# One core, a hybrid encoder layer: the order of splits, gates and tables around the first two expert blocks

## The reference

```
def block_fn(args):
    tok, w, e = args
    xb = h_pad[tok]                                    # 128 rows of one expert
    gu = xb @ w_gate_up[e]                             # 1024 x 1024
    y = (jax.nn.silu(gu[:, :D_EXPERT]) * gu[:, D_EXPERT:]) @ w_down[e]   # 512 x 1024
    return y * w[:, None]
```

## Time and profile before

| | |
|---|---|
| median of 3 runs | 1258.5 us (1257.77 to 1258.85) |
| the profiled execution | 1256.18 us, span 1254.5 us, granted clock 0.991 |
| TensorE matmuls busy | 1220.5 us, 97% of the span |
| VectorE / ScalarE / GpSimd busy | 904.5 / 610.1 / 218.6 us |
| chain that ended last | PE 91%, DVE 3%, DMA 2%, issue 2% |

### The profile page before, as it was taken

One profiled execution on the slowest core, in us unless ns is written; L12 is line 12 of the kernel. 1 busy time (PEld: TensorE's weight loads), 2 busy tenths in 40 slices (PEclk: granted clock), 3 DMA queues, 4 the chain that ended last, 5 costly groups with the idle time before them and its releaser, 6 DMA issues.

```text
span 1254.5 us, 25280 instructions
## 1 busy us (share of the span) xinstructions
PE 1220.5 (97%) x7475; PEld 1007.7 (80%) x7476; DVE 904.5 (72%) x1137; ACT 610.1 (49%) x665; POOL 218.6 (17%) x281
## 2 busy tenths in 40 slices
PE   5999999999999999999999999999999999999897
PEld 4889999998888865788888888888888888888653
DVE  2546345667999888856887566745889888998497
ACT  3331111131222244647775565645777877787433
POOL 0042311000111111211121111111121221222122
PEclk8999999999999999999999999999999999999999
DMA  9944411046333578767998666955999999998994
GB/s 313 303 140 128 124 48 35 18 135 184 123 115 131 193 287 314 317 257 284 373 402 346 263 260 247 344 221 210 384 405 400 397 395 400 388 401 303 342 404 165
DMA packets 122710, 329.21 MB, mean 262 GB/s; under 512 B 12888, under 2 KB 44704, under 8 KB 122660
## 3 DMA queue, kind: packets, MB, share of 16 engines
q1 hardware_dynamic: 107700, 288.08, 61.6%
q0 software_dynamic: 13088, 34.13, 7.7%
q10 hardware_dynamic: 1872, 6.29, 1.3%
HBM read 296.97 MB, written 39.39 MB: 268 GB/s over the span
## 4 chain that ended last, share of the span: by engine, by line
PE 91%; DVE 3%; DMA 2%; issue 2%; SPq 1%; ACT 1%; POOL 0%; POOLq 0%; DVEq 0%; ACTq 0%
PE bank L1668 22%; PE bank L1670 22%; PE bank L1669 22%; PE bank L1681 4%; PE bank L1683 4%; PE bank L1682 3%; PE bank L1983 3%; PE bank L1898 1%; PE bank L2100 1%; PE bank L2099 1%; PE bank L2023 1%; PE bank L1737 1%; PE bank L1764 1%; PE bank L1728 1%; PE bank L1876 1%
## 5 line engine op out<-in xcount | busy, mean ns | idle before, releaser
L1510 DVE TENSOR_TENSOR gu_l<-gu_raw,gu_h (+1 forms) x128 | 287.3, 2285 | 40.7 <-ACT gu_h L995 27.5
L995 ACT ACTIVATE gu_h<-gu_raw (+1 forms) x128 | 239.1, 1927 | 12.5 <-issue 8.8
L1668 PE MATMUL bank<-gu_h,xT_h 128*128 x608 | 240.3, 395 | 1.3 <-DVE xT_l L1536 1.3
L1670 PE MATMUL bank<-gu_h,xT_l 128*128 x608 | 237.1, 390 | 0.0
L1669 PE MATMUL bank<-gu_l,xT_h 128*128 x608 | 236.5, 389 | 0.0
L1514 DVE TENSOR_TENSOR dn_l<-dn_raw,dn_h (+1 forms) x64 | 143.6, 2285 | 6.7 <-issue 5.0
L1668 PEld LDWEIGHTS bank<-gu_h,xT_h 128*128 128x128 f32 x608 | 114.2, 188 | 24.2 <-issue 2.0
L1670 PEld LDWEIGHTS bank<-gu_h,xT_l 128*128 128x128 f32 x608 | 114.1, 188 | 24.3
L1669 PEld LDWEIGHTS bank<-gu_l,xT_h 128*128 128x128 f32 x608 | 114.3, 188 | 22.6
L1668 PE MATMUL bank<-dn_h,aT_h 128*128 (+1 forms) x308 | 123.2, 400 | 0.0
L1681 PE MATMUL bank<-hT_h,win_h 128*128 128x256 f32 x384 | 110.6, 288 | 11.5 <-DVE hT_l L1188 10.4
(11 more groups left out here) (313 smaller groups left out, 2069.8 us busy)
## 6 DMA issues: line engine op xcount, KB each, us to landing
gu_raw<-in_w_gate_up SPq DMA_DIRECT2D x128, 1024.0 KB, 7.4
dn_raw<-in_w_down SPq DMA_DIRECT2D x64, 1024.0 KB, 7.3
y<-y_rows SPq DMA_DIRECT2D x22, 512.0 KB, 7.3
ada_raw<-in_w_ada SPq DMA_DIRECT2D x20, 512.0 KB, 7.6
ada_raw<-in_w_ada SPq DMA_DIRECT2D x10, 1024.0 KB, 5.5
win_raw<-in_w_in SPq DMA_DIRECT2D x8, 768.0 KB, 9.0
h_rows<-h SPq DMA_DIRECT2D x12, 512.0 KB, 2.7
fin<-x_rows SPq DMA_DIRECT2D x12, 512.0 KB, 9.9
```

What stands on the lines that cost most here:

```text
L995: nc.scalar.activation(gu_slot(gu_h, e, c), gu_slot(gu_raw, e, c), ACT.Copy).then_inc(S["gu_split_h"], 1)
L1510: nv.tensor_tensor(gu_slot(gu_l, e, c), gu_slot(gu_raw, e, c), gu_slot(gu_h, e, c).bitcast(F32), ALU.subtract).then_inc(S["gu_split_l"], 1)
L1668: mm(out, lh, rh, start=start, stop=False)
L1670: return mm(out, ll, rh, start=False, stop=stop)
```

## The change

Four things are done. TensorE turns block 1's rows behind chunk 1 of block 0 and no longer behind chunk 2. In block 0 chunk 3 of the next expert is split before `silu`/`gate` and no longer behind. In block 1 VectorE splits chunk 2 of the next expert behind `gate` and `low_xT`; `scatter_table()` moves from behind `low_xT(2)` to behind the two `low_dn`, and `weights()` behind the whole loop. The tile `x0T_h` starts 64 bytes later.

```diff
--- before.py
+++ after.py
@@ -305,7 +305,7 @@
         aT_h = r.take("aT_h", [P, KE, P], F32R)
         aT_l = r.take("aT_l", [P, KE, P], F32R)
         WT0 = r.at
-        x0_at = C0 + 17728
+        x0_at = C0 + 17792
         r = Region(x0_at)
         x0T_h = r.take("x0T_h", [P, KD, P], F32R)
         x0T_l = r.take("x0T_l", [P, KD, P], F32R)
@@ -1062,13 +1062,14 @@
                     act.wait_ge(S["x1_stored"], 16 * NT)
                     high_xT(1)
                     with act.If(e < e_next):
-                        high_gu(e_next, 2)
+                        for c in (2, 3):
+                            high_gu(e_next, c)
                     act.wait_ge(S["g2_added"], 16)
                 silu(i)
                 if not first:
                     high_xT(i + 1)
-                with act.If(e < e_next):
-                    high_gu(e_next, 3)
+                    with act.If(e < e_next):
+                        high_gu(e_next, 3)
                 if first:
                     for c in range(2):
                         high_dn(0, c)
@@ -1567,21 +1568,19 @@
             def expert_block(i, first=False, second=False):
                 e, e_next = expert_of(i), expert_of(i + 1)
                 with dve.If(e < e_next):
-                    for c in range(2 if first else 3):
+                    for c in range(2 if first or second else 3):
                         low_gu(e_next, c)
                 if first:
                     low_xT(1)
                     with dve.If(e < e_next):
-                        low_gu(e_next, 2)
+                        for c in (2, 3):
+                            low_gu(e_next, c)
                 gate(i)
                 if not first:
                     low_xT(i + 1)
-                if second:
-                    scatter_table()
-                with dve.If(e < e_next):
-                    low_gu(e_next, 3)
-                if second:
-                    weights()
+                    with dve.If(e < e_next):
+                        for c in ((2, 3) if second else (3,)):
+                            low_gu(e_next, c)
                 if first:
                     for c in range(2):
                         low_dn(0, c)
@@ -1589,12 +1588,15 @@
                     with dve.If(expert_of(i - 1) < e):
                         for c in range(2):
                             low_dn(e, c)
+                if second:
+                    scatter_table()
                 low_aT(i)
 
             expert_block(0, first=True)
             expert_block(1, second=True)
             with dve.Fori(2, n_blocks) as i:
                 expert_block(i)
+            weights()
 
             last_block = dve.value_load(block_n[0:1, 1:2], min_val=NE - 1, max_val=MAXBLK - 1)
             last_col = dve.value_load(block_c[0:1, bass.ds(last_block, 1)], min_val=0, max_val=COLS - 1)
@@ -1995,7 +1997,7 @@
                             kk = 2 * c + k
                             last = three(ps[5 + b][:], x0T_h[:, kk, :], x0T_l[:, kk, :], w_h[:, k, n], w_l[:, k, n], kk == 0, kk == KD - 1)
                     last.then_inc(S["gu_used"], 1)
-                    if c == 2:
+                    if c == 1:
                         x_transposes(1)
 
             def gate_up(i, e, chunks=range(4)):
```

## The result

After the change the median is 1263.78 us (1262.01 to 1266.14, 7 runs); the kernel before, run beside it, stands at 1258.5 us (1254.49 to 1260.73, 7 runs). The ratio is 1.0045 with a 95% interval of 1.0029 to 1.0061: 5.7 us slower (3.6 to 7.7). The forecast was 1268.2 us within 1263.5 to 1271.5. The direction and the place were right, the size was too large: the time lies 0.3 us inside the low end.

A forecast was written before the change was run, and what follows sets the result against it. TensorE, busy 97% of the span, was taken to bound the kernel. To the median of 1258.5 us were added 5.6 (table), 1.9 (clock) and 2.2 (tail), 9.7 in all: 1268.2 us, range 1263.5 to 1271.5.

The forecast's parts named there:

- the case without a low clock: Rival: same wait ahead of block 1's down matmuls, clock stays high, tail free; 1264.3 us, chance 0.06.
- the anchor: The forecast's starting point: 1258.5 us, the median of before, 2.3 us above its profiled execution of 1256.18.
- Entry wait: Loop entry: TensorE's 1.30 us wait for block 2's xT_l goes away, as xT_l ends at 514.83.
- Gathered rows: Block 0: block 1's gathered rows land at 490.9, before TensorE needs them at 491.8; no cost.
- Scatter table, +5.6: Block 1: table ends 6.6 us later, at 526.53, so the down matmuls start 5.6 us later, at 535.54.
- the 0.24 us of the tile: Moving x0T_h's start by 64 bytes saves 5 ns on each of 48 matmuls, 0.24 us.
- Clock, +1.9: Behind the new wait TensorE runs at 1.2 GHz for 3.73 us and loses 1.9 us.
- Weights in the tail, +2.2: Tail: GpSimd holds the second operation of weights(), so the tail's first matmul starts 2.2 us later.
- free tail: Rival: same wait and low clock, but GpSimd doesn't hold the tail's small operations, 0.2 us there; 1266.2 us, chance 0.27.

The follow-up runs named there:

- tables_late: Kernel before with scatter_table() and weights() moved behind the two low_dn of block 1, ahead of low_aT(1), nothing else; ratio to before 1.0045, 1263.22 us.
- after_free: Kernel after with the clearing write given its own zeros and semaphore, so take_y(0) doesn't wait for it; ratio to before 1.0008, 1257.62 us.
- turn_only: Kernel before with x_transposes(1) behind chunk 1 in place of chunk 2, nothing else; ratio to before 0.9993, 1257.28 us.
- warm: Kernel after with block 2 written out in TensorE's program and its 8 row transposes made seven times; ratio to before 1.0024, 1262.18 us.
- weights_only: Kernel before with weights() moved behind the loop, nothing else; ratio to before 1.0000, 1258.22 us.
- after_again: The unchanged kernel after, measured once more beside the variants; ratio to before 1.0046, 1262.91 us.
- table_back: Kernel after with scatter_table() alone put back behind low_xT(2), ahead of the splits of chunks 2 and 3; ratio to before 1.0011, 1259.72 us.
- table_mid: Kernel after with scatter_table() behind the splits of chunks 2 and 3, ahead of block 1's two low_dn; ratio to before 1.0023, 1261.9 us.
- order_only: Kernel before with only the split of expert 2's chunk 2 moved behind low_xT(2) and the scatter table; ratio to before 1.0015, 1259.0 us.

## Why the prediction was right in direction and high in size

The mechanism was right at its main place and wrong in the tail. That the time lies inside the range is in part luck: the low end stood under the case without a low clock (1264.3), and that isn't what happened. Of the 4.4 us by which the forecast was high, 2.5 come from its terms, above all the tail's, and 1.9 from the anchor.

- **What bounds it.** Right. The loss lies at one place, ahead of block 1's down matmuls, and the late scatter table is its cause: `tables_late` makes it without the rest of the change, `after_free` takes it away with the table still late.
- **Entry wait.** Right in the trace (gone), with `xT_l` of block 2 ending at 515.88 rather than 514.83, because the last chunk of expert 2 started on ScalarE at 511.18 and not at 510.19. The text had named that 1.0 us as the price if the load came late.
- **Gathered rows.** Wrong. The gather was to land at 490.9 and TensorE wasn't to wait; it waited 1.00 us. The issue took 3.17 us instead of the 1.06 us of the kernel before, and VectorE's split had begun just ahead of it, at 485.83. In `turn_only` the same stands (3.18 us, a wait of 1.24). In the kernel after it cost nothing in the end: TensorE came to the down matmuls 1.0 us later and waited 1.0 us less there.
- **Scatter table, +5.6.** Measured 5.2. The steps were forecast one by one: table ends 526.53 (measured 527.40), copy of 0.18 us (0.18), write issued 528.35 (529.22), `take_y(0)` 532.35 (532.55), down matmuls 535.54 (535.14). VectorE's 0.9 us of lateness was mostly made good between the issue and ScalarE's start: 3.33 us where I took 4.0. The last step was wrong: TensorE followed `aT_l` by 0.29 us and not by the 0.89 of the loop's entry, 0.6 us less. Those 0.29 us stood in the rows, but were read as a margin of the table; it had none. The wait was 5.8 us, not 7.2, by these 0.4 us and since TensorE arrived at 529.3 instead of 528.4, with the gathered rows late and without the 0.24 us of the tile.
- **Clock, +1.9.** Measured 2.2 in the kernel after, and 2.2 by `warm`. Right. The Trainium skill says in "TensorE: Matmul & The Clock Gate", Part 1, that an idle array falls to 1.2 GHz and that work brings the 2.4 GHz back; here the trace agrees, with a granted clock of 0.50 behind 5.8 us of idle time and of 1.00 again from 540 us on, behind work.
- **Weights in the tail, +2.2.** This is the step that failed, the term of the sum that was mis-sized: measured -0.3 in the tail, and 1.0000 for `weights_only`. I had set the second operation at 1175.7 against the CAST of the earlier trace rows, at a GpSimd write that would be under way. In fact the five operations run directly behind the last `aT_l`, and GpSimd's write there was issued 0.26 us after the second of them had started. The rival "free tail" named this case and gave 1266.2.
- **The anchor.** The two profiled executions differ by 7.2 us, the medians by 5.3. The 7.2 are the 5.2 + 2.2 of the place, less 0.3 in the tail. Adding to the median of before presumed that its profiled execution, 2.3 us below that median, is like the others; the one of after was only 0.4 us below. With the forecast's first two terms alone, 7.5 us, the median would have been 1266.0, still 2.2 us above the measured one. What the other executions of the kernel before do in those 2 us isn't in the one trace of it, and stays open. Two other things bear on it. In the traces of `weights_only` and `turn_only`, kernels of the same time as before by their ratios, block 2's activation transposes stand at 536.80 and 537.82 and not at 535.51: the trace of before is an early one at this very place. And the executions differ in granted clock: of the 25 of the kernel before beside `after_again`, the six with 0.987 took 1259.33 to 1262.22 us and the three with 0.992 took 1254.06 to 1256.74. The profiled one had 0.991.
- **The table's early place.** The text took the 5.6 us as the length by which the table is late, less the margin. `table_back`, `table_mid` and `order_only` show that this holds for the late place and not between the places: each time the followers of an earlier table were slower, by 1.3 to 1.8 us in the copy and by 1.2 to 3.9 us from the issue's start to the landing, 1.2 us of them in the issue itself. The start of `take_y(0)` was 527.34 in the earlier trace rows, 529.07 in `table_back`, 529.54 in `order_only`, 531.72 in `table_mid` and 532.55 after, for tables that ended at 519.92, 518.77, 520.02, 523.54 and 527.40.

## What to carry to other kernels

An operation with little to do can carry a long tail: five operations of 2.8 us in all held TensorE for 5.8 us and 2.2 us of clock behind them, since a DMA, an index copy and another engine's buffer hung on their end. Look at what waits for the step that is moved, and free that (a source and a semaphore of its own) rather than look for a better place in the queue. A gain at one wait is worth nothing while the next one, 12 us on, has no margin. A few tenths of a microsecond between the end of one engine's work and the start of the next can be the release itself: see how long it is where the second engine was surely waiting, before calling it slack.

## What the runs showed of the hardware

- The issue of an indirect DMA on GpSimd isn't of fixed length. In all traces from block 0 to the loop's end it took 0.96 to 1.06 us where no split (`TENSOR_TENSOR` of 128x2048, both inputs in SBUF) was under way on VectorE, and 2.1 to 3.2 us where it began within a split and more than 0.3 us ahead of its end. There is one exception: in `tables_late` an issue that began 0.03 us behind a split's start took 1.06 us. The Trainium skill says in "SBUF — State Buffer", Who interferes with whom, that such an operation takes the shared pair's read interface only, and infers that the generation of descriptors, which needs the write interface, isn't stalled by it. Here the whole issue instruction was longer (3.17, 2.23, 2.22 and 2.12 us in the lines above). It has an index in SBUF to read. Which part of it waits, the reading of the index or the descriptors, no run here tells apart, so what the page infers is neither borne out nor refuted.
- An indirect write of 128 rows of 4 KB landed 3.26 us behind the start of its issue with the DMA engines idle (kernel after), 4.45 us with the issue longer by 1.2 us and the engines nearly idle (`table_mid`), 4.98 us with a short issue beside loads of weights (`turn_only`), and 6.35 and 7.13 us with both (`order_only`, `table_back`). A gather of the same size took 8.70 us beside loads, with an issue of 1.01 us (`after_free`).
- Where TensorE had waited 4.15 to 5.81 us for `aT_l`, the granted clock was low for a stretch behind it (0.50 in the windows above, 0.57 in the same window of `table_mid`), at a price of 2.2 us (kernel after), 2.4 (`after_again`, `tables_late`) and 1.6 (`table_mid`), by the time from the down matmuls to block 2's activation transposes less the 5.58 us of the kernel before. The price didn't follow the length of the wait: 4.15 us in `tables_late` cost more than 4.71 us in `table_mid`. Behind the 2.25 us of `order_only` the clock stayed at 1.00.
- Matmuls on a stationary tile went from 395 to 390 ns (the first of each three from 405 to 400) when the tile's start moved from 17792 to 17920 bytes behind its region's start; the step from 17728 to 17792 had changed nothing.
